# A hybrid decoder step on one core: another order for the small work between the projection jobs

## The reference, cut to what matters

```python
h, gate_ada = ada_norm(x, c, norm_g, w_ada, b_ada)          # shift, scale, gate = silu(c) @ w_ada + b_ada
f, nsa_rows, win_rows, dsa_rows, idx_rows = in_projection(h, w_in, pos)
ck = silu((blocks of cached and new keys + pe) @ cmp_w1[0]) @ cmp_w2[0]     # and cv with index 1
o_n = nsa_attend(...)      # compressed, selected and window branch
score = where(causal, sum_h relu(idx_q . idx_k) * idx_w, NEG)
_, sel = top_k(score, topk)                                 # 128 of up to 512 keys, 65 of 260 for samples
o_d = dsa_attend(...)      # attention over the selected keys alone
y = x + gate_ada * ((sigmoid(m_n) * (o_n * silu(z_n)) @ w_up_nsa + ...) @ w_out)
```

## Time and profile before

| | us |
|---|---|
| median of 3 runs | 620.12 (618.89 to 623.26) |
| the profiled execution | 620.08 |
| its span, first to last instruction | 618.2 |

### The profile page before, as it was taken

The page is one execution under the profiler, slowest core; times in us unless marked ns, Lnnn a source line. Parts: engine busy times, 40 slices in busy tenths (PEclk is TensorE's granted clock), DMA queues, the critical chain, the costliest instruction groups (busy, mean ns, idle before and its releaser), DMA issues.

```text
span 618.2 us, 12162 instructions
## 1 busy us (share of the span) xinstructions
PE 588.5 (95%) x4630; PEld 483.5 (78%) x4630; DVE 338.3 (55%) x847; ACT 248.0 (40%) x549; POOL 152.0 (25%) x196
## 2 busy tenths in 40 slices
PE   5999999998999999999999999999999999999995
PEld 1587776765776887766775679999999999998784
DVE  1454035968878556878676664433232542227873
ACT  6232255232131345666466554343213232223443
POOL 1126350450350445553554430000000000000130
PEclk9799999999799999999999999999999999999998
DMA  9991731521342264001201306328332242333003
GB/s 321 385 323 31 295 114 39 165 65 56 108 139 83 73 173 139 2 1 50 88 2 49 91 1 169 105 69 268 116 69 70 84 122 69 89 117 137 1 28 118
DMA packets 52426, 68.37 MB, mean 111 GB/s; under 512 B 5089, under 2 KB 34969, under 8 KB 52208
## 3 DMA queue, kind: packets, MB, share of 16 engines
q1 hardware_dynamic: 49744, 56.85, 30.0%
q10 hardware_dynamic: 1808, 6.31, 2.8%
q0 software_dynamic: 816, 4.43, 1.8%
HBM read 62.99 MB, written 6.66 MB: 113 GB/s over the span
## 4 chain that ended last, share of the span: by engine, by line
PE 82%; DVE 9%; SPq 2%; issue 2%; ACT 2%; DMA 2%; POOL 1%; DVEq 0%; ACTq 0%; POOLq 0%
PE psum L1161 30%; PE psum L934 8%; PE psum L936 7%; PE psum L935 7%; PE psum L1423 3%; PE psum L1346 3%; PE psum L1391 3%; PE psum L1261 3%; PE psum L960 2%; PE psum L1068 2%; DVE psum L2079 2%; PE psum L949 1%; DVE score L2003 1%; SPq L714 1%; DVE top L2002 1%
## 5 line engine op out<-in xcount | busy, mean ns | idle before, releaser
L1551 ACT ACTIVATE w_hi<-stage 128x1024 fp32r<-128x1024 f32 (+2 forms) x56 | 56.1, 1002 | 160.5 <-PE psum L1161 93.9
L1893 DVE TENSOR_TENSOR w_lo<-stage,w_hi 128x1024 fp32r<-128x1024 f32 x34 | 41.7, 1225 | 110.5 <-ACT w_hi L1551 107.2
L1161 PE MATMUL psum<-hT_hi,w_hi 128*128 128x272 f32 x368 | 76.4, 289 | 0.0
L1161 PE MATMUL psum<-hT_lo,w_hi 128*128 128x272 f32 x368 | 76.2, 288 | 0.0
L1161 PE MATMUL psum<-hT_hi,w_lo 128*128 128x272 f32 x368 | 75.9, 288 | 0.0
L934 PE MATMUL psum<-w_hi,hT_hi 128*128 128x512 f32 (+3 forms) x192 | 70.3, 366 | 0.7 <-DVE rope_b L1940 0.4
L844 POOL TENSOR_TENSOR w_lo<-stage,w_hi 128x1024 fp32r<-128x1024 f32 (+2 forms) x22 | 44.2, 2011 | 108.6 <-ACT w_hi L1551 108.6
L936 PE MATMUL psum<-w_lo,hT_hi 128*128 128x512 f32 (+3 forms) x192 | 67.4, 351 | 0.0
L935 PE MATMUL psum<-w_hi,hT_lo 128*128 128x512 f32 (+3 forms) x192 | 67.4, 351 | 0.0
L925 POOL TENSOR_TENSOR y<-y,final_g 128x512 f32<-128x512 f32 (+1 forms) x5 | 7.8, 1581 | 217.7 <-ACT merged L1781 217.7
L1161 PEld LDWEIGHTS psum<-hT_hi,w_hi 128*128 128x128 f32 x368 | 57.8, 188 | 0.4 <-DVE w_lo L1893 0.2
(11 more groups left out here) (346 smaller groups left out, 1123.4 us busy)
## 6 DMA issues: line engine op xcount, KB each, us to landing
stage<-in_w_in SPq DMA_DIRECT2D x14, 1024.0 KB, 5.2
stage<-in_w_ada SPq DMA_DIRECT2D x8, 1024.0 KB, 10.3
stage<-in_w_in SPq DMA_DIRECT2D x10, 512.0 KB, 5.2
staging<-in_x_prompt ACTq DMA_DIRECT2D x4, 512.0 KB, 5.4
cached<-in_cache_nsa_kv SPq DMA_DIRECT2D x32, 64.0 KB, 2.2
stage<-in_cache_nsa_kv SPq DMA_DIRECT2D x16, 128.0 KB, 2.1
stage<-in_state_nsa_win_kv SPq DMA_DIRECT2D x2, 1024.0 KB, 6.4
stage<-in_cache_dsa_kv SPq DMA_DIRECT2D x16, 128.0 KB, 2.1
```

The source lines that it names most:

```text
L1161: last = mm(out[:, h, :], left[w][:, k, P * x:P * x + P], halves(mov[m])[:, h, :], start=(k == 0 and w + m == 0), stop=(k == tiles - 1 and ...
L1551: last = A(dst, src, ACT.Copy)
L1893: last = tt(dst, src, hi.bitcast(F32), ALU.subtract)
```

## The change

In job 2 the four `ikT` entries move ahead of `cmpT`, `k` and `kn`. In jobs 3 and 4 a `raw` entry and a query entry take turns (new function `queries_and_rows`), with the emptying engines exchanged so that each engine has every second entry. `hid` moves behind `mod`, just ahead of `modT`. `ck` goes from job 3 to the head of job 4, and `cvp` and `cvs` go from job 4 to job 5. In DVE's `aux` the calls `rounds(2, 8)`, and `rounds(2, 4)` with `rounds(3, 4)`, stood ahead of the waits for `ck` and `cvp`; they now stand behind the copies of `modT` (4,1) and `modT` (5,0). Nothing is added or taken away.

```diff
--- before.py
+++ after.py
@@ -84,11 +84,17 @@
         for j in pairs:
             add(at, "q", (which, j), "av"[j % 2])
 
+    def queries_and_rows(at, which, s):
+
+        for n in range(4):
+            add(at, "raw", (s, n), "av"[n % 2])
+            add(at, "q", (which, n), "va"[n % 2])
+
     for kind, n, e in (("mod", (4, 0), "a"), ("qi", 0, "a"), ("modT", (4, 0), "v"), ("qi", 1, "v"), ("ki", 0, "a"),
                        ("si", 0, "v")):
         add(1, kind, n, e)
-    for kind, n, e in (("cmpT", 0, "v"), ("cmpT", 1, "a"), ("k", SLC, "a"), ("kn", SLC, "v"), ("ikT", 0, "a"),
-                       ("ikT", 1, "v"), ("ikT", 2, "a"), ("ikT", 3, "v")):
+    for kind, n, e in (("ikT", 0, "a"), ("ikT", 1, "v"), ("ikT", 2, "a"), ("ikT", 3, "v"), ("cmpT", 0, "v"),
+                       ("cmpT", 1, "a"), ("k", SLC, "a"), ("kn", SLC, "v")):
         add(2, kind, n, e)
     for t in (1, 2, 3):
         for h in range(4):
@@ -96,23 +102,19 @@
             if (t, h) == (1, 1):
                 add(2, "sdots", 0, "a")
     add(2, "ssum", 0, "v")
+
     queries(3, PLAIN, range(4))
     add(3, "qs", PLAIN, "v")
-    queries(3, ROT, range(2))
-    for n in range(4):
-        add(3, "raw", (0, n), "av"[n % 2])
-    queries(3, ROT, range(2, 4))
-    for kind, n, e in (("qs", ROT, "v"), ("hid", 0, "a"), ("mod", (4, 1), "a"), ("ck", 0, "v"), ("modT", (4, 1), "v")):
+    queries_and_rows(3, ROT, 0)
+    for kind, n, e in (("qs", ROT, "v"), ("mod", (4, 1), "a"), ("hid", 0, "a"), ("modT", (4, 1), "v")):
         add(3, kind, n, e)
-    queries(4, DSAQ, range(2))
-    for n in range(4):
-        add(4, "raw", (1, n), "av"[n % 2])
-    queries(4, DSAQ, range(2, 4))
-    for kind, n, e in (("qs", DSAQ, "v"), ("hid", 1, "a"), ("mod", (5, 0), "a"), ("cvp", 0, "v"), ("cvs", 0, "a"),
-                       ("cvs", 1, "v"), ("modT", (5, 0), "v")):
+    add(4, "ck", 0, "v")
+    queries_and_rows(4, DSAQ, 1)
+    for kind, n, e in (("qs", DSAQ, "v"), ("mod", (5, 0), "a"), ("hid", 1, "a"), ("modT", (5, 0), "v")):
         add(4, kind, n, e)
-    for kind, n, e in (("mod", (5, 1), "a"), ("selx", 0, "a"), ("selx", 1, "a"), ("modT", (5, 1), "v"),
-                       ("grow", 0, "v"), ("grow", 1, "v"), ("k", WIN, "a"), ("kn", WIN, "v")):
+    for kind, n, e in (("mod", (5, 1), "a"), ("cvp", 0, "v"), ("cvs", 0, "a"), ("modT", (5, 1), "v"), ("cvs", 1, "v"),
+                       ("selx", 0, "a"), ("selx", 1, "a"), ("grow", 0, "v"), ("grow", 1, "v"), ("k", WIN, "a"),
+                       ("kn", WIN, "v")):
         add(5, kind, n, e)
     return aux
 
@@ -1974,12 +1976,12 @@
                             cp(dst, part_t).then_inc(*tell(aux_dve))
                         else:
                             tt(dst, dst, part_t, ALU.add).then_inc(*tell(aux_dve))
+                        if n == (4, 1):
+                            rounds(2, 8)
+                        elif n == (5, 0):
+                            rounds(2, 4)
+                            rounds(3, 4)
                         continue
-                    if kind == "ck":
-                        rounds(2, 8)
-                    elif kind == "cvp":
-                        rounds(2, 4)
-                        rounds(3, 4)
                     dve.wait_ge(aux_done, i + 1)
                     if kind == "ssum":
                         tt(scoreS[:, :], src[0:NS, 0:NKS], tb("midx", NS), ALU.add).then_inc(*tell(aux_dve))
```

## The result

The changed kernel has a median of 637.83 us in four executions (635.67 to 643.61), the kernel before 620.55 us in the four beside them (618.89 to 623.26). The ratio is 1.029, with a 95% interval of 1.0251 to 1.0328: slower by 16 to 20 us. The forecast was 641 with a range of 634 to 649.

A forecast was written before the change was run, and what follows sets the result against it. PE was taken to bound the kernel, busy 95% of the span, with DVE having next to no slack in job 3. Moved work and late readings +16.1 and clock +5 gave 21 us on 620.1, 641 us, range 634 to 649.

The forecast's parts named there:

- the part of the clock: Half clock behind PE's waits for DVE (1.5 and 2.5 us) and ahead of hid (1): together +5, bounds 0 and +13.
- reading of job 3: DVE's reading ahead of job 4 starts at 180.8 instead of 172.59, +8.2, behind 26.8 us of search.
- rival (a): Jobs 3 and 4: the moved rounds find room in DVE's slack, the kernel is not slower, 619.4; 5 in 100.
- the samples' search: Job 3, DVE: 11.88 us (155.53 to 167.41), counted within the 26.8 us of search behind the modT copy.
- PE waits about 1 us: Job 3: PE waits about 1 us for its second half of weights, issued at 152.5 and split from 157.5.
- PE's waits for DVE sum to under 8: Sign that the prediction is wrong: PE's waits for DVE sum to under 8 us; forecast 8 to 9 and 6.
- the reading's start: Sign, ahead of job 4: the prediction is wrong if reading starts before 178; forecast 180.8.
- These cost nothing under the 9: Job 3: PE's wait of about 1 us for later weights is covered by its 9 us wait for DVE.
- (b): Jobs 3 and 4: only one of the two blocks of rounds runs over, 632; 5 in 100.
- (c): Jobs 4 and 5: the clock stays down through the small work, half of a hid at 1.2 GHz, 650; 12 in 100.
- The price of 2.6 us for one episode: Loss taken for one half-clock episode, from job 3's 154.40 to 161.05: a piece took 8.3 us, others 5.65.
- I take 0: Job 2: same transposes and copies in another order, 0, with bounds of -0.4 and +0.5.

The follow-up runs named there:

- b1: The kernel before with only DVE's rounds of jobs 3 and 4 moved behind the modT copies, entries in old order: 638.63 us, ratio 1.0298.
- d1: The kernel before with the new order of job 2 alone, ikT entries first: 621.88 us, ratio 1.0034.
- a1: The changed kernel with DVE's rounds of jobs 3 and 4 put ahead of the waits for modT: 626.14 us, ratio 1.0102.
- d4: a1 with hid's weights loaded into a separate place, qT_idx and kz_idx, instead of the staging buffer: 619.87 us, ratio 0.9987.
- a2: The changed kernel with only rounds(2, 8) ahead of its modT wait, job 4's rounds still behind modT: 631.85 us, ratio 1.0198.
- c2: a1 with hid ahead of mod again in jobs 3 and 4, modT last: 627.19 us, ratio 1.0093.
- b2: The kernel before with ck and modT at the head of job 4, modT, cvp, cvs of job 5, rounds behind the last query copy: 620.76 us, ratio 1.0005.
- b4: b3 with the samples' matmuls of projection jobs' second weight halves ahead of PE's wait for POOL's low part: 620.22 us, ratio 0.9997.
- c1: The kernel before with only the turns of raw and query entries in jobs 3 and 4: 622.18 us, ratio 1.0026.
- d3: b3 with hid's weights loaded into qT_idx and kz_idx instead of the staging buffer: 618.49 us, ratio 0.9967.
- d2: The kernel before with DVE's mask of the samples' scores moved behind the four rounds that follow it: 619.48 us in one execution.
- b3: The kernel before with only ck and modT (4,1) at the head of job 4, rounds(2, 8) behind job 3's last query copy: 620.04 us, ratio 0.9991.

## Why the prediction was right, and where it was off

Direction and mechanism held, and b1 shows the mechanism alone. The size held too, slower by 17 to 18 us against 21 forecast and inside the range, but the part of the clock in it by luck. In the table the second column is what the forecast had, the third the profile after, counted from a start of job 3 that is 5.7 later.

| Step | forecast | measured |
|---|---|---|
| job 2 | 0 | +4.9 in this execution, by clock; +1.4 by medians (d1) |
| `hid` 0 begins | 143.2 | 148.97 - 5.72 = 143.25 |
| DVE idle ahead of the `modT` copies | about 10 | 10.71, 11.68 |
| block of search, job 3 and job 4 | 26.8, 17.1 | 24.6, 17.1 |
| reading of job 3 | +8.2 | 184.26 - 5.72 - 172.59 = +5.95 |
| reading of job 4 | +14.3 | 228.86 - 5.72 - 211.31 = +11.8 |
| PE waits for weights | about 1 in job 3; in job 4 none but under rival (a) | 2.73, 2.12 |
| PE waits for DVE | 9, 6 | 3.48, 4.05 |
| half clock at 155 to 161 | gone | gone |
| small work of job 5 begins | +14.1 | 235.06 - 5.72 - 216.19 = +13.15 |
| second layers in job 5 | +2.0 | +1.9 |
| clock | +5, behind the waits and ahead of `hid` | +4.3: 1.3 behind the second wait, 3.0 from 240 to 247 |
| first attention unit begins | | 257.00 - 5.72 - 233.25 = +18.0 |
| sum from job 3 on | +21 | +17.9 |

**The mis-sized term** is the samples' search, "11.88 (155.53 to 167.41)". It was taken from a row as work and carried to a place beside other neighbours. Its last 2.54 us were an instruction that waited for POOL, and at the new place it takes 0.30. The 2.24 us less explain the reading exactly (8.2 - 5.95 = 2.25) and go through all later steps: +11.8 for +14.3. From there the forecast had +1.8 for the small tiles and the second layers and, outside its steps, +5 for the clock; the profile has +6.1.

**PE's waits** were shorter than forecast with the same start of the reading. "PE waits about 1 us" for weights was taken from the shift of the load, but the wait stands ahead of the samples' matmuls (1.08), and `hid`'s end to the low part took some 9.1 us and not 8.6. So 2.7 us of the wait for DVE are called a wait for weights, and the half clock behind it stretches PE's work into more. This changed the names of the waits and not the time: PE went on when DVE had read. The criterion "PE's waits for DVE sum to under 8" would have called the mechanism wrong by 7.5 though it held; the reading's start, 178.5 against the limit of 178, was the better one, and also near. The idle time of the waiting engine is a poor test where several waits share the same cover.

**"These cost nothing under the 9"** held in the changed kernel and hid a cost. a1 shows what lay beneath, 6 us, and so rival (a) would hardly have been 619.4 as worked out but nearer to a1's 626: its two waits for weights were 4.8 us and not 2, and the clock fell behind the first of them and under `hid` 1. With the buffer freed (d4) it is 619.87, which is rival (a)'s number by another way.

**Rivals.** (b), only one block runs over, is excluded: a2 gives 6.0 to one and 5.7 to the other. (c), the clock stays down through a `hid`, did not happen in the profile: both `hid` took 9.31. In a1 and c2 it did for a part of `hid` 1 (10.75 and 10.97). The rule that VectorE runs its queue in order held in every timeline here.

**The clock** came out near the forecast by luck (+4.3 against +5), in other places than forecast. Behind the first wait the forecast had 1.5 us. But the kernel after is 5.95 us late at the reading of job 3 and 5.4 at job 4's small work (191.59 - 5.72 - 180.44), and the forecast lost the same 0.6 there (8.2 to 7.6) without any clock, so nothing was paid. Ahead of `hid` it had 1, and both `hid` took their full-clock 9.31. Behind the second wait it had 2.5, and the small tiles took 1.3 more. The other 3.0 us lie in a stretch that the forecast has no place for, at the end of job 5's small work. The kernel after, PE's timeline and windows view:

```profile
240.89 1.11 PE L1176 MATMUL psum<-tab,staging 128*128 128x128 f32 x4
```

```profile
242.00:250.00 8.00, 8.00 (x55) 7.61 (x55) 5.89 (x13) 1.86 (x3) 2.57 (x2) 0.68 0.09 24
```

The four transposes take 0.66 in the kernel before. From the row ahead of them to the samples' matmuls behind them (240.11 to 247.44) PE takes 7.33 us, before 4.35 (219.34 to 223.69). No wait of PE stands in the 5 us ahead, only thin work. Job 5 has such a stretch in six of the fourteen profiles (the kernel after, b1, b2, b4, c1, d3), four of them with the old order of job 5's entries, so it isn't the mark of this change.

The price of 2.6 us for one episode came from one profile too. From the end of `modT` to the samples' matmuls PE takes 8.3 us in it (155.32 to 163.60), but 7.1 to 7.2 in b1, c1, d1 and d2, which have the same entries there. A difference of 1 us between two profiles says nothing here. "I take 0" for job 2 had nothing for the clock; d1 puts +1.4 on it by medians, and the 643.61 of the profiled execution has 4.9 of it. Not settled: why the clock falls in such a stretch in one execution and not in another, as no kernel has a profile of each kind.

## What to carry to other kernels

Long filler work on an engine with an in-order queue belongs ahead of a wait and not behind it, when the work that follows it is itself waited for: a copy of 0.2 us that waited for another engine kept 10 us of search from a slot it had filled, and the next job paid. Before costing such a move, take the neighbours into account: a duration can hold a wait for another engine, and a wait that lies "hidden" under a longer one is still there when that one is mended. The load that waits for a buffer wasn't helped by another order around it (b2, b3, b4, c2 gained nothing), but by another place for what holds the buffer (d3, d4).

## What the runs showed of the hardware

A DVE instruction can be held by a running POOL instruction with no semaphore between them, and the profile counts this as busy. The same mask of 32x288 took 0.30 us with no split running (the kernel after, b1, d2), 2.54 from 164.95 beside a split that ended at 167.32, and 1.14 in a1, where DVE's and POOL's timelines read:

```profile
163.78 1.14 DVE L2014 TENSOR_SCALAR score_sample<-score_sample 32x288 f32<-32x288 f32 x1
```

```profile
160.09 4.66 POOL L846 TENSOR_TENSOR w_lo<-stage,w_hi 128x1024 fp32r<-128x1024 f32 x2 [24.39 <-ACT w_hi L1553]
```

POOL ends at 164.75 and the mask at 164.92, 0.17 behind, as in the kernel before. In a2 and c1 it took 1.25 and 1.42, each time ending 0.15 behind a split. In c2 it began 0.01 us ahead of one, at 167.29, and took 0.30, and the split took 2.57 instead of 2.41. The samples' MAX8, 0.45 us each, took no longer beside the same split (L2004 at 160.51 and 161.53 of a1). The Trainium skill, "SBUF — State Buffer", section "SBUF: two separate sides", says that VectorE and GpSimd have a pair of ports in common that works as a lock: a VectorE instruction in a two-port mode, or with two inputs in SBUF beside a GpSimd instruction that reads SBUF, and a GpSimd instruction exclude each other for a whole instruction. The trace agrees as far as it goes: the mask and the split excluded each other, whichever began first, and the MAX8, with one input in SBUF, did not wait. In which mode the mask ran no row shows.

Of the clock: a wait of 1.23 us with thin work around it was followed by 6.65 us at 1.2 GHz. The 2.65 ahead of the samples' matmuls in a1 were followed by 1.91 us for matmuls that take 1.08 at full clock, and the 2.12 in job 4 of the kernel after by 1.92 for such as take 1.07. But behind 2.02 in b2, 2.17 in a2 and 2.19 in a1 the same matmuls took 1.07 or 1.08, and the clock stayed up. In job 5 of c1 it fell at 221.8 though PE had no wait since 213.24. So the length of the single wait did not decide it in these runs.
